# The scans' solve on two diagonal blocks, on opposite quarters of the array

## The chip, the cores and the metric

One core of one Trainium2 chip runs the kernel. The metric is the device time of one execution, in microseconds. The kernel before took 3053.93 us (median of three runs, 3050.66 to 3057.09).

## The reference, cut to what matters

The reference is a two-layer backbone over 512 tokens (256 of context, 256 latent), 1024 wide, in fp32. Each layer projects its input, runs four token mixers, merges them and applies a feed-forward part (dense in layer 0, eight experts in layer 1). One of the four mixers scans the tokens with a state of 64 x 64 for each of four heads, once forward and once backward:

```python
def step(state, inp):
    r_t, w_t, k_t, v_t, a_t, b_t = inp
    sa = jnp.einsum('bhvk,bhk->bhv', state, a_t)
    state = (state * w_t[:, :, None, :] + sa[..., None] * b_t[:, :, None, :]
             + v_t[..., None] * k_t[:, :, None, :])
    return state, jnp.einsum('bhvk,bhk->bhv', state, r_t)
```

Only this scan is touched. The context's tokens are scanned first; layer 1 needs outputs y of the latent tokens alone.

## The kernel before, in words

The scan is done in chunks of 128 tokens: 4 chunks by 2 directions give the 8 groups of a layer, 16 in the kernel. In a chunk the token's dependence on earlier tokens of the same chunk is a strictly triangular 128 x 128 matrix A for each head, and what is wanted is the inverse of 1 - A, applied to a right side of 64 columns. A is split into "near" (blocks of 16 on the diagonal, D) and "far" (the rest, E0). The inverse of the near part is a product of powers, F = (1+D)(1+D^2)(1+D^4)(1+D^8), and that of what is left is G = (1+Z)(1+Z^2)(1+Z^4), with Z the far part times F. The vectors u0 (right side), u1 = F u0 and u = G u1 follow from the state of the chunk before; from u follow the next state and the outputs y.

All of it is written out by hand, as one fixed order of instructions on each of three engines, with a semaphore value for each step (`done`/`tick`). The four heads are numbered p + 2q: p picks 64 of 128 partitions where a head is an operand's rows, and one of two banks of PSUM where it is an output, so that most steps come twice, for p = 0 and p = 1.

- TensorE (`solve`, line 689; all matrix products stand in the trace under line 465, the transposes under 745): the gram products of the chunk (bank 0/1: b with a and r; bank 4/5: a with b; bank 2/3: k with a and r, after `carry_u0` of the group before); then D^2, D^4 and F2, D^8 and F3, F4, four transposes of b and k, Z, Z^2, Z^4 and G2, G3. Between these stand the steps of the group before: `carry_u0` (line 622), `carry_u1`, `carry_u` and `carry_state` (state and y). `four` multiplies two heads of one p, 128 x 128 by 128 x 128. One fp32 product is two MATMUL records in the trace, each with a weight load of its own.
- VectorE (`solve`, line 1891): masks of the gram products (lines 1907 to 1919, with 1912 for 1 + D), the sums of F and G (line 1925), 1 + Z (line 1945), the copies of u0 and u, the state (lines 1872, 1873), the output y (lines 1885, 1887). In groups 0 to 3 it also prepares the second direction (`sums`, `rates`, `hats`), in groups 6 and 7 it splits weights for the stage after.
- ScalarE (`solve`, line 1389): copies of every squared matrix from PSUM to SBUF, one per p (128x512 for D^2, D^4, Z, Z^2; 128x256 for D^8, Z^4), the turned b and k, and u1; the exponentials of the second direction after groups 1 and 2.

SyncE loads the weights in order through a ring of four units; three of its units serve as scratch until `hats` of the second direction. What follows the scans (`attention_in`) waits for "group end" of group 7. The masks come with the constants, 128 x 128 each.

## Time and profile before

| what | value |
|---|---|
| time, median of three runs | 3053.93 us |
| the profiled execution's own time | 3055.04 us |
| its span in the trace | 3053.2 us |
| TensorE busy, whole span | 2920.9 us (96%) |
| scans of layer 0 | 111 to 313 us of the span |
| scans of layer 1 | 1368 to 1558 us of the span |
| in the 202 us of layer 0's scans: TensorE, VectorE, ScalarE busy | 192.57, 121.79, 66.75 us |

The profile is one execution. "Busy" counts an engine's instructions; of TensorE the weight loads are listed apart (PEld), and they overlap the products. PEclk is the share of full clock that TensorE was granted: 1.00 is 2.4 GHz, 0.50 is 1.2 GHz. The time outside the two scans is not touched by the change.

### The profile page before, as it was taken

The page shows a single profiled execution, that of the slowest core. Times are in us where ns is not written, and L with a number is a line of the kernel's source. Part 1 is how long each engine was busy: PE and PEld are TensorE (multiplying, and loading weights), DVE is VectorE, ACT ScalarE, POOL GpSimd, SP SyncE. Part 2 cuts the span into 40 slices and gives each one's busy share as a digit, 9 for nine tenths or more (in the row PEclk, how much of TensorE's full clock was granted, in tenths as well). Part 3 has the DMA queues.
Part 4 walks back from the last instruction along what each step waited for, and adds up shares of the span by engine and source line. Part 5 has one row for each costly group of instructions (what it writes and reads, how often), then busy time and mean ns, then how long its engine had stood idle before and what let it go on. Part 6 is the DMA issues. An engine that isn't in the chain of part 4 may idle for free.

```text
span 3053.2 us, 43457 instructions
## 1 busy us (share of the span) xinstructions
PE 2920.9 (96%) x16364; PEld 2406.1 (79%) x16364; DVE 1980.7 (65%) x2592; ACT 1577.7 (52%) x2073; POOL 0.2 (0%) x4
## 2 busy tenths in 40 slices
PE   7999999999899999899999898999999999999997
PEld 4788676787688878669887797888888888888886
DVE  3765575335422233476556556988988889888887
ACT  5433446223322222353344544777777777777775
POOL 0000000000000000000000000000000000000000
PEclk8999999999999999999999998999999999999999
DMA  6010136223122222200114454899998999989995
GB/s 254 1 43 1 55 140 222 95 97 118 70 97 97 97 83 97 83 14 1 43 42 160 174 181 167 339 351 354 352 347 342 355 356 349 348 341 355 357 348 212
DMA packets 79820, 575.53 MB, mean 188 GB/s; under 512 B 8896, under 2 KB 10176, under 8 KB 10176
## 3 DMA queue, kind: packets, MB, share of 16 engines
q1 hardware_dynamic: 78960, 568.49, 49.4%
q10 hardware_dynamic: 720, 5.08, 0.4%
q8 instruction: 99, 1.62, 0.2%
q14 instruction: 41, 0.34, 0.0%
HBM read 572.49 MB, written 1.05 MB: 188 GB/s over the span
## 4 chain that ended last, share of the span: by engine, by line
PE 86%; DVE 8%; ACT 3%; issue 2%; DMA 0%; DVEq 0%; ACTq 0%; SPq 0%
PE bank L465 84%; PE bank L1122 1%; PE bank L961 1%; ACT weights_high L1213 1%; DVE weights_low L2179 1%; ACT hT L1213 1%; DVE weights_low L1720 1%; ACT more_weights_high L1213 1%; ACT arena L1213 1%; DVE arena L1992 1%; DVE arena L1763 0%; DVE arena L1925 0%; DMA xT<-xin 0%; DVE arena L1696 0%; DVE arena L1750 0%
## 5 line engine op out<-in xcount | busy, mean ns | idle before, releaser
L1213 ACT ACTIVATE arena<-bank 128x512 f32<-128x512 f32 (+2 forms) x647 | 310.9, 491 | 871.0 <-PE bank L465 780.8
L1213 ACT ACTIVATE weights_high<-ring 128x1024 fp32r<-128x1024 f32 (+1 forms) x366 | 508.5, 1397 | 313.2 <-PE bank L465 312.7
L1720 DVE TENSOR_TENSOR weights_low<-ring,weights_high 128x1024 fp32r<-128x1024 f32 x220 | 266.2, 1224 | 399.4 <-ACT weights_high L1213 399.3
L465 PE MATMUL bank<-arena 128*128 128x128 f32 (+6 forms) x3632 | 453.4, 297 | 23.1 <-DVE arena L1925 6.0
L465 PEld LDWEIGHTS bank<-arena 128*128 128x128 f32 (+3 forms) x3632 | 390.1, 182 | 64.8 <-issue 23.8
L2179 DVE TENSOR_TENSOR weights_low<-ring,weights_high 128x2048 fp32r<-128x2048 f32 x146 | 334.6, 2292 | 66.1 <-ACT weights_high L1213 65.8
L465 PE MATMUL bank<-h_low,weights_high 128*128 128x512 f32 (+1 forms) x960 | 348.3, 363 | 0.0
L465 PE MATMUL bank<-weights_high,tokens_high 128*128 128x512 f32 x684 | 276.2, 404 | 7.2 <-DVE weights_low L2179 5.5
L465 PE MATMUL bank<-weights_high,tokens_low 128*128 128x512 f32 x684 | 267.6, 391 | 0.0
L2179 DVE TENSOR_TENSOR more_weights_low<-arena,weights_high 128x2048 fp32r<-128x2048 f32 x108 | 247.6, 2292 | 30.5 <-ACT weights_high L1213 30.3
L1213 ACT ACTIVATE weights_high<-arena 128x2048 fp32r<-128x2048 f32 x108 | 207.0, 1917 | 44.7 <-PE bank L465 44.7
L465 PE MATMUL bank<-weights_low,tokens_high 128*128 128x512 f32 x576 | 224.5, 390 | 0.0
L465 PEld LDWEIGHTS bank<-h_low,weights_high 128*128 128x128 f32 x960 | 182.8, 190 | 27.0
L465 PE MATMUL bank<-h_high_ffn,weights_high 128*128 128x512 f32 x448 | 176.0, 393 | 10.1 <-DVE h_low L1727 10.1
L465 PE MATMUL bank<-h_high_gates,weights_high 128*128 128x512 f32 (+1 forms) x512 | 174.0, 340 | 9.0 <-DVE h_low L1727 9.0
L2179 DVE TENSOR_TENSOR weights_low<-ring,more_weights_high 128x2048 fp32r<-128x2048 f32 x73 | 167.4, 2293 | 18.7 <-ACT more_weights_high L1213 18.5
L465 PE MATMUL bank<-h_high_ffn,weights_low 128*128 128x512 f32 x448 | 175.0, 391 | 0.0
L465 PE MATMUL bank<-h_high_gates,weights_low 128*128 128x512 f32 (+1 forms) x512 | 173.0, 338 | 0.0
L465 PE MATMUL bank<-more_weights_low,tokens_high 128*128 128x512 f32 x432 | 168.5, 390 | 0.0
L465 PEld LDWEIGHTS bank<-weights_high,tokens_high 128*128 128x128 f32 x684 | 128.4, 188 | 36.0 <-DVE weights_low L2179 9.3
L1213 ACT ACTIVATE more_weights_high<-ring 128x2048 fp32r<-128x2048 f32 x73 | 139.8, 1915 | 26.2 <-PE bank L465 26.2
L465 PEld LDWEIGHTS bank<-weights_high,tokens_low 128*128 128x128 f32 x684 | 128.3, 188 | 27.9
(282 smaller groups left out, 5439.9 us busy)
## 6 DMA issues: line engine op xcount, KB each, us to landing
ring<-wstream SPq DMA_DIRECT2D x377, 1024.0 KB, 4.8
arena<-wstream SPq DMA_DIRECT2D x162, 1024.0 KB, 4.8
sm<-small ACTq DMA_DIRECT2D x2, 1568.0 KB, 8.8
xT<-xin SPq DMA_DIRECT2D x1, 2048.0 KB, 9.4
cn<-consts ACTq DMA_DIRECT2D x1, 1732.0 KB, 7.0
out<-hT SPq DMA_DIRECT2D x2, 512.0 KB, 3.0
vec<-vecs SPq DMA_DIRECT2D x1, 121.5 KB, 2.4
cn<-consts ACTq DMA_DIRECT2D x1, 65.0 KB, 2.5
```

Source lines behind the costliest of these rows:

```text
L465: return nc.tensor.matmul(o, lhsT, rhs, start=first, stop=last)
L961: ins = nc.tensor.transpose(bank[4 + s][:, b * P:(b + 1) * P], T(PB[n % 3 * 2 + s])[:, b * P:(b + 1) * P], C("ident"))
L1122: ins = nc.tensor.transpose(bank[5 - 3 * (p % 2)][:, c * P:(c + 1) * P], ghid[:, p % 2, c * P:(c + 1) * P], C("ident"))
L1213: return nc.scalar.activation(o, i, func, **kw)
L1720: step(vx.tensor_tensor(ring_low[:, u % RING, cols], ring[:, u % RING, cols], wh[:, j % 4, :].bitcast(F32), ALU.subtract), "weights low", j)
L1992: chain(vx.reciprocal(r, r))
L2179: return vx.tensor_tensor(low, raw, moe_high(q).bitcast(F32), ALU.subtract)
```

## The change

The chunk's matrix is taken as two by two blocks of 64. Only the two diagonal blocks of a head are inverted, and the block that couples the second half of the tokens to the first is applied apart.

- `four` now takes all four heads: for each head and each half s, 64 x 64 by 64 x 64, with operands on the partitions of half s and the output on the same partitions. That is 8 products instead of 2 (4 over both p), and all tiles hold the four heads side by side, so each step has one wait, one copy and one sum in place of two (by p).
- In a block of 64 the series of G ends one factor earlier: Z^4 and G3 are gone, and Z^2 is made in one orientation.
- The gram products a with b are made in 64 x 64 pieces, 16 of them in both orientations, and 4 more for the coupling block C; b with r and k with a, r stay as they are. They are issued at the end of the group before (`gram_blocks`).
- New on TensorE: FC (F times C), W (FC times G), and the product of W with the first half of u (`carry_across`), whose result VectorE adds to the second half of u. u1 and u are made with 8 products of 64 x 64 each, not 4 of 128 x 128. G2 of a group is made at the start of the next group's `solve`.
- ScalarE copies C, FC and W (64 partitions), and one tile each for D^2, D^4, D^8, Z, Z^2.
- The output y goes to bank 1 and is made after FC, apart from the state; VectorE takes it in the next but one `solve`. `sums` is cut in two parts, and `hats` now stands before 1 + Z ("G1") of groups 2 and 3 instead of behind it.
- The masks near and far are 64 wide, and a 64 x 64 identity on both halves is new.

The core of the diff, with lines that only rename or move left out:

```diff
-        def half_tiles(i):
-            return T(i, 2).rearrange("p a (k h t) -> p a k h t", k=2, h=2)
-        DD = half_tiles(M_)
-        D2 = half_tiles(M_ + 2)
-        FG_of = (half_tiles(FG_), half_tiles(FG_ + 2))
-        AR2_of = (half_tiles(AR2_), half_tiles(AR2_ + 2))
...
-        E0 = two_halves(E0_)
-        E1_of = (two_halves(E1_), two_halves(E1_ + 1))
-        D8 = two_halves(D8_)
+        def whole(i):
+            return T(i).rearrange("p (h t) -> p h t", h=4)
+        def blocks(i):
+            return T(i).rearrange("p (k h t) -> p k h t", k=2, h=4)
+        DD, D2, FW = blocks(M_), blocks(M_ + 1), blocks(M_ + 2)
+        FG_of = (blocks(FG_), blocks(FG_ + 1))
+        EC, D8 = blocks(E0_), blocks(D8_)[:, 0]
+        E1_of = (whole(E1_), whole(E1_ + 1))
+        AR2_of = ((whole(AR2_), whole(AR2_ + 1)), (whole(AR2_ + 2), whole(AR2_ + 3)))
+        def ends(d):
+            return (rows(0), rows(1)) if d == 0 else (rows(1), rows(0))
         bk_of = (T(BK_), T(BK_ + 1))
...
-            def four(o, left, right, kind):
-                for q in range(2):
-                    ins = mm(o[:, (2 * kind + q) * P:(2 * kind + q + 1) * P], left[:, q, :], right[:, q, :])
+            def four(o, left, right):
+                for h in range(4):
+                    for s in range(2):
+                        ins = mm(o[rows(s), h * HD:(h + 1) * HD], left[rows(s), h, :], right[rows(s), h, :])
+                return ins
+            def across(o, to, left, right, of):
+                for h in range(4):
+                    ins = mm(o[to, h * HD:(h + 1) * HD], left[of, h, :], right[of, h, :])
                 return ins
...
-                        ins = mm(bank[6 + p][:, P + q * HD:P + (q + 1) * HD], FG_of[m % 2][:, p, 0, q, :], u0[:, p, q, :])
+                        for s in range(2):
+                            ins = mm(bank[6 + p][rows(s), P + q * HD:P + (q + 1) * HD],
+                                     FG_of[m % 2][rows(s), 0, 2 * p + q, :], u0[rows(s), p, q, :])
...
+            def carry_across(l, m):
+                first, second = ends(groups[m][0])
+                pe.wait_ge(*done("W", l, m))
+                for p in range(2):
+                    pe.wait_ge(*done("u", l, m, p))
+                    for q in range(2):
+                        ins = mm(bank[6 + p][second, P + q * HD:P + (q + 1) * HD], FW[first, 1, 2 * p + q, :],
+                                 uu[first, p, q, :])
+                    ins.then_inc(*tick(products, "u across product", l, m, p))
...
+            def gram_blocks(l, n):
                 d, c = groups[n]
-                cols = slice(c * CH, (c + 1) * CH)
-                FG = FG_of[n % 2]
+                first, second = ends(d)
+                def of_chunk(part_):
+                    return slice(c * CH + part_.start, c * CH + part_.stop)
                 if n % 4 == 0:
                     pe.wait_ge(*done("hats", l, d, 1))
                 if n == 0:
                     pe.wait_ge(*done("rate read", l, 1, 1))
+                for kind in range(2):
+                    for q in range(2):
+                        for p in range(2):
+                            for s in range(2):
+                                a, b = ar_of[d][rows(p), q, c, 0, rows(s)], bh(d, q)[rows(p), of_chunk(rows(s))]
+                                at = 2 * kind + q
+                                ins = mm(bank[4 + p][rows(s), at * HD:(at + 1) * HD], *((b, a) if kind else (a, b)))
+                ins.then_inc(*tick(products, "gram", l, n))
+                if n:
+                    pe.wait_ge(*done("bk", l, n - 1))
+                    pe.wait_ge(*done("FC", l, n - 1))
                 for q in range(2):
                     for p in range(2):
-                        mm(bank[p][:].rearrange("p (s q t) -> p q s t", s=2, q=2)[:, q], bh(d, q)[rows(p), cols],
-                           ar_of[d][rows(p), q, c, :, :])
+                        ins = mm(bank[2 + p][second, (4 + q) * HD:(5 + q) * HD], ar_of[d][rows(p), q, c, 0, second],
+                                 bh(d, q)[rows(p), of_chunk(first)])
+                ins.then_inc(*tick(products, "gram across", l, n))
...
+            def last_power(l, n):
+                pe.wait_ge(*done("Z2", l, n))
+                pe.wait_ge(*done("G1", l, n))
+                four(bank[0][:, 256:512], D2[:, 1], FG_of[n % 2][:, 1]).then_inc(*tick(products, "G2 product", l, n))
+            def across_second(l, n):
+                first, second = ends(groups[n][0])
+                pe.wait_ge(*done("G2", l, n))
+                pe.wait_ge(*done("FC", l, n))
+                across(bank[3], first, FW[:, 0], FG_of[n % 2][:, 1], second).then_inc(*tick(products, "W product", l, n))
+            def solve(l, n):
+                d, c = groups[n]
+                first, second = ends(d)
+                FG = FG_of[n % 2]
+                cols = slice(c * CH, (c + 1) * CH)
+                if n == 0:
+                    gram_blocks(l, 0)
+                else:
+                    last_power(l, n - 1)
+                    carry_u0(l, n - 1)
+                pe.wait_ge(*done("masked D", l, n))
+                pe.wait_ge(*done("C", l, n))
+                four(bank[4][:, 0:256], DD[:, 1], DD[:, 0])
+                four(bank[4][:, 256:512], DD[:, 0], DD[:, 1]).then_inc(*tick(products, "D2 product", l, n))
+                if n:
+                    across_second(l, n - 1)
+                    carry_u1(l, n - 1)
+                pe.wait_ge(*done("D2", l, n))
+                four(bank[5][:, 0:256], D2[:, 1], D2[:, 0])
+                four(bank[5][:, 256:512], D2[:, 0], D2[:, 1]).then_inc(*tick(products, "D4 product", l, n))
+                pe.wait_ge(*done("F1", l, n))
+                four(bank[4][:, 256:512], D2[:, 0], FG[:, 0]).then_inc(*tick(products, "F2 product", l, n))
+                if n >= 2:
+                    pe.wait_ge(*done("group end", l, n - 2))
                 for q in range(2):
                     for p in range(2):
+                        ins = mm(bank[p][:, q * P:(q + 1) * P], bh(d, q)[rows(p), cols], ar_of[d][rows(p), q, c, 1, :])
+                ins.then_inc(*tick(products, "gram r", l, n))
                 if n:
+                    pe.wait_ge(*done("W", l, n - 1))
                 for q in range(2):
                     for p in range(2):
                         ins = mm(bank[2 + p][:, 2 * q * P:2 * q * P + 2 * P], kh(d, q)[rows(p), cols],
                                  ar_of[d][rows(p), q, c, :, :])
+                ins.then_inc(*tick(products, "gram k", l, n))
                 if n:
                     carry_u(l, n - 1)
+                pe.wait_ge(*done("D4", l, n))
+                pe.wait_ge(*done("F2", l, n))
+                four(bank[4], DD[:, 1], DD[:, 0]).then_inc(*tick(products, "D8 product", l, n))
+                four(bank[5], DD[:, 0], FG[:, 0]).then_inc(*tick(products, "F3 product", l, n))
                 if n:
+                    carry_across(l, n - 1)
+                pe.wait_ge(*done("D8", l, n))
+                pe.wait_ge(*done("F3", l, n))
+                four(bank[4][:, 256:512], D8, FG[:, 0]).then_inc(*tick(products, "F4 product", l, n))
+                pe.wait_ge(*done("masked k", l, n, 0))
                 for i in range(4):
                     ins = nc.tensor.transpose(bank[2][:, i * P:(i + 1) * P],
                                               (bh(d, i) if i < 2 else kh(d, i - 2))[:, cols], C("ident"))
                 ins.then_inc(*tick(products, "bk turned", l, n))
+                if n:
+                    carry_state(l, n - 1)
+                pe.wait_ge(*done("F4", l, n))
+                four(bank[5][:, 0:256], EC[:, 0], FG[:, 0])
+                four(bank[5][:, 256:512], FG[:, 0], EC[:, 0]).then_inc(*tick(products, "Z product", l, n))
+                pe.wait_ge(*done("masked k", l, n, 1))
+                across(bank[3], second, FG[:, 0], EC[:, 1], second).then_inc(*tick(products, "FC product", l, n))
+                if n:
+                    carry_y(l, n - 1)
+                pe.wait_ge(*done("Z", l, n))
+                pe.wait_ge(*done("masked r", l, n))
+                four(bank[0], DD[:, 0], DD[:, 1]).then_inc(*tick(products, "Z2 product", l, n))
+                if n < 7:
+                    gram_blocks(l, n + 1)
...
+                def across(n):
+                    _, second = ends(groups[n][0])
+                    act.wait_ge(*done("gram across", l, n))
+                    for p in range(2):
+                        ins = f(EC[second, 1, 2 * p:2 * p + 2], bank[2 + p][second, 256:384]
+                                .rearrange("p (q t) -> p q t", q=2), ACT.Copy)
+                    ins.then_inc(*tick(scalars, "C", l, n))
+                def across_second(n):
+                    first, _ = ends(groups[n][0])
+                    copy(FW[first, 1], by_head(3, 0, first), ("W", "W product"), n)
                 def solve(n):
+                    _, second = ends(groups[n][0])
+                    if n == 0:
+                        across(0)
+                    copy(D2, both_kinds(4), ("D2", "D2 product"), n)
                     if n:
+                        across_second(n - 1)
                         carry_u1(n - 1)
+                    act.wait_ge(*done("F1", l, n))
+                    copy(DD, both_kinds(5), ("D4", "D4 product"), n)
+                    copy(D8, by_head(4), ("D8", "D8 product"), n)
                     act.wait_ge(*done("bk turned", l, n))
                     if n == 0:
                         act.wait_ge(*done("hats", l, 0, 1))
                     if n >= 2 and n != 5:
                         act.wait_ge(*done("state product", l, n - 2, 1))
                     f(bk_of[n % 2], bank[2][:], ACT.Copy).then_inc(*tick(scalars, "bk", l, n))
+                    copy(DD, both_kinds(5), ("Z", "Z product"), n)
+                    copy(FW[second, 0], by_head(3, 0, second), ("FC", "FC product"), n)
+                    copy(D2[:, 1], by_head(0), ("Z2", "Z2 product"), n)
+                    if n < 7:
+                        across(n + 1)
...
+            def mask_blocks(l, n):
+                up, low = ways(groups[n][0])
+                dve.wait_ge(*done("gram", l, n))
+                if n:
+                    dve.wait_ge(*done("G1", l, n - 1))
+                for p in range(2):
+                    own_heads = slice(2 * p, 2 * p + 2)
+                    x = bank[4 + p][:, 0:256].rearrange("p (k q t) -> p k q t", k=2, q=2)
+                    vx.tensor_tensor(DD[:, 0, own_heads], x[:, 0], mask("near" + low, HD, 2), ALU.mult)
+                    vx.tensor_tensor(DD[:, 1, own_heads], x[:, 1], mask("near" + up, HD, 2), ALU.mult)
+                    vx.tensor_tensor(EC[:, 0, own_heads], x[:, 0], mask("far" + low, HD, 2), ALU.mult)                        .then_inc(*tick(vectors, "masked D", l, n))
+                dve.wait_ge(*done("masked D", l, n))
+                step(vx.tensor_tensor(FG_of[n % 2][:, 0], DD[:, 1], mask("eye64"), ALU.add), "F1", l, n)
...
             def solve(l, n):
+                if n == 0:
+                    mask_blocks(l, 0)
+                else:
+                    add(l, n - 1, 1, 0, 256, "G2")
                     carry_u0(l, n - 1)
+                if n >= 2:
+                    carry_y(l, n - 2)
+                if n < 2:
+                    running_sums(l, 1, n)
+                add(l, n, 0, 4, 256, "F2")
+                mask_r(l, n)
+                mask_k(l, n, 0)
                 if n:
                     carry_u(l, n - 1)
+                add(l, n, 0, 5, 0, "F3")
+                if n:
+                    carry_across(l, n - 1)
+                add(l, n, 0, 4, 256, "F4")
+                mask_k(l, n, 1)
+                if n < 2:
+                    centred_sums(l, 1, n)
+                elif n < 4:
+                    rates(l, 1, n - 2)
+                    hats(l, 1, n - 2)
+                elif n >= 6:
+                    weights_low(LAYER_START[l] + ATT_AT + 2 * n - 10)
+                dve.wait_ge(*done("Z", l, n))
+                step(vx.tensor_tensor(FG_of[n % 2][:, 1], DD[:, 0], mask("eye64"), ALU.add), "G1", l, n)
                 if n:
                     carry_state(l, n - 1)
+                if n < 7:
+                    mask_blocks(l, n + 1)
```

## Rows read from the trace of the kernel before

**Rows 1.** The page, parts 1 and 4: busy time by engine, chain by engine.
```profile
PE 2920.9 (96%) x16364; PEld 2406.1 (79%) x16364; DVE 1980.7 (65%) x2592; ACT 1577.7 (52%) x2073; POOL 0.2 (0%) x4
...
PE 86%; DVE 8%; ACT 3%; issue 2%; DMA 0%; DVEq 0%; ACTq 0%; SPq 0%
```

**Rows 2.** Busy time by window (us, records); both layers' scans, then three short stretches.
```profile
core 0: us, PE busy (x) PEld busy (x) DVE busy (x) ACT busy (x) POOL busy (x), PEclk, DMA share, GB/s
111.00:313.00 202.00, 192.57 (x1729) 174.08 (x1729) 121.79 (x333) 66.75 (x133) 0.00 (x0) 0.96 0.04 17
1368.00:1559.00 191.00, 183.57 (x1634) 168.03 (x1635) 117.90 (x325) 67.55 (x134) 0.00 (x0) 0.97 0.05 18
...
112.00:116.00 4.00, 4.00 (x24) 2.89 (x21) 1.65 (x6) 0.00 (x0) 0.00 (x0) 0.50 0.00 0
...
300.00:313.00 13.00, 11.08 (x74) 8.91 (x73) 3.66 (x11) 1.13 (x5) 0.00 (x0) 0.68 0.00 1
1537.47:1539.47 2.00, 2.00 (x35) 1.42 (x36) 0.58 (x2) 0.05 (x1) 0.00 (x0) 1.00 0.00 0
```

**Rows 3.** Timeline (start us, length us): first mask of groups 5 and 6.
```profile
232.02 0.42 DVE L1907 TENSOR_TENSOR arena<-bank,cn 128x256 f32<-128x256 f32 x1 [1.15 <-PE bank L465]
...
255.97 0.42 DVE L1907 TENSOR_TENSOR arena<-bank,cn 128x256 f32<-128x256 f32 x1 [1.15 <-PE bank L465]
```

**Rows 4.** Groups of instructions by form, 231 to 255 us (busy, mean ns, idle before).
```profile
L465 PE MATMUL bank<-arena 128*128 128x128 f32 x120 | 15.0, 280 | 0.5 <-DVE arena L1925 0.5
L1213 ACT ACTIVATE arena<-bank 128x512 f32<-128x512 f32 x9 | 5.4, 597 | 14.4 <-PE bank L465 10.3 <-PE bank L745 4.1
L1925 DVE TENSOR_TENSOR arena<-arena,bank 128x256 f32<-128x256 f32 x10 | 4.1, 420 | 6.5 <-PE bank L465 6.4
...
L1213 ACT ACTIVATE arena<-bank 128x256 f32<-128x256 f32 x4 | 1.5, 384 | 2.2 <-PE bank L465 2.2
```

**Rows 5.** Timeline of weight loads in group 5, a load beside each product record.
```profile
231.65 0.31 PEld L465 LDWEIGHTS bank<-state,arena 64*128 64x128 f32 x4
...
232.02 0.52 PEld L465 LDWEIGHTS bank<-arena 128*128 128x128 f32 x4
...
232.61 0.30 PEld L465 LDWEIGHTS bank<-state,arena 64*128 64x128 f32 x4
...
237.30 2.76 PEld L465 LDWEIGHTS bank<-arena 128*128 128x128 f32 x24
...
239.98 0.97 PEld L465 LDWEIGHTS bank<-u,arena 128*128 128x128 f32 x8
...
242.87 0.20 PEld L465 LDWEIGHTS bank<-uu,arena 128*64 128x64 f32 x4
...
243.48 0.19 PEld L465 LDWEIGHTS bank<-arena,state 64*64 64x64 f32 x4
...
243.84 0.20 PEld L465 LDWEIGHTS bank<-arena,uu 128*64 128x64 f32 x4 [0.17 <-issue]
...
244.43 0.19 PEld L465 LDWEIGHTS bank<-arena,state 64*64 64x64 f32 x4 [0.17 <-issue]
...
245.39 0.97 PEld L465 LDWEIGHTS bank<-arena 128*128 128x128 f32 x8 [0.17 <-issue]
```

**Rows 6.** The same view at the gram products of group 6.
```profile
254.29 1.39 PEld L465 LDWEIGHTS bank<-arena 64*128 64x128 f32 x16
255.60 0.19 PEld L465 LDWEIGHTS bank<-state,arena 64*128 64x128 f32 x2
```

**Rows 7.** Timeline in group 2: the end of `hats`, TensorE's next load.
```profile
179.71 0.68 DVE L1840 TENSOR_TENSOR arena<-ring 128x512 f32<-128x512 f32 x1
...
180.92 0.75 PEld L465 LDWEIGHTS bank<-arena 128*128 128x128 f32 x6 [1.80 <-ACT ring L1213]
```

**Rows 8.** TensorE's sequencer at two waits (lines 763, 630), first and last start us.
```profile
L763 PEldq EVENT_SEMAPHORE  x1: 51/51/51, 253.6 to 253.6; - x1
...
L630 PEldq EVENT_SEMAPHORE  x1: 51/51/51, 254.3 to 254.3; - x1
```

210 lines of the change are left out of this document (71 added, 139 removed), and 2 rows, old and new, of the table _n.

## The prediction

> **What bounds the kernel now.** First the page: TensorE is busy 96% of the span and holds 86% of the chain that ended last [rows 1]. Then the windows of the two scans: of 202 us in layer 0 TensorE is busy 193, VectorE 122, ScalarE 67, and layer 1 looks alike [rows 2]. So inside the scans, too, time goes by TensorE's work. Then the pace: from the first mask of one group to that of the next 255.97 - 232.02 = 23.95 us [rows 3]. By form, 120 of a group's records are 128 x 128 by 128 x 128, and TensorE sits idle 0.5 us before them, while ScalarE waits 14.4 us and VectorE 6.5 us for TensorE [rows 4]. The reader should see that these two are the followers, and have room.
>
> **The unit costs**, by start to start of weight loads:
> - A record over the full array: 24 of them from 237.30 to 239.98, 0.112 us each [rows 5].
> - The outputs of y: 4 records of 64*64 in 243.84 - 243.48 = 0.36, then 8 of 128*64 in 0.59 [rows 5]. The second stretch has two pairs more, so a pair with 128 columns costs 0.11 and a change of layout (which part of the array a weight fills) 0.36 - 0.22 = 0.14. The four 64*64 loads stand within 0.19 us: the two opposite quarters run side by side, like the column halves.
> - 16 records of 128*64 with 64 columns take 243.48 - 242.87 = 0.61, less one change 0.47 for eight pairs: 0.059 a pair [rows 5]. I call that a slot.
> - u0: twice 232.61 - 231.65, 1.92, with four changes in it [rows 5]. Sixteen gram records 1.31: four pairs of 128 columns 0.44, so four pairs of 256 columns 0.87 [rows 6].
>
> On a change of layout the Trainium skill, "TensorEngine Tiling (Array Packing)", section "Key Properties", says that changing the mode drains the array; it gives no price, and the 0.14 above is what it costs here.
>
> **A group before**, on TensorE: 136 full records (120 of the solve, 16 of u1 and u) 15.2; u0 1.92; gram products 0.44 + 0.87 + 0.87; four transposes 0.44; state 0.61; y with its changes 1.91; three more changes 0.4: 22.7. The other 1.3 of 23.95 are waits and edges.
>
> **A group after.** Slots with two quarters: G2 8, D^2 16, u1 8, D^4 16, F2 8, u 8, D^8 8, F3 8, F4 8, Z 16, Z^2 8, gram blocks 16, coupling gram 4: 132. Steps on one quarter alone (W, FC, the product across) are 24 records, each of which I price as a slot too, since each column half above advanced by one record in 0.059. Nothing in the trace shows one quarter alone; bounds are 0.03 (it pairs with a neighbour) and 0.112 (a full record), and the half-width row is the nearest. So 156 slots, 9.2 us. No row has this form with 64 columns either: for the 132 the lower bound is 0.055 (half of the 0.11 for 128 columns) and the upper one two full records, 0.224; I take 0.059, because the same-width weights of rows 5 show it and because the quarters ran side by side there.
> Kept: u0 1.92, gram r 0.44, gram k 0.87, transposes 0.44, state 0.47 without its change, y 1.91: 6.05. Layout changes not in these: into u0, into and out of the r and k grams, into the transposes, into the state, into Z and one for the edge of a 128-wide load: 7 x 0.14 = 1.0. Sum 16.25 us, 6.4 less than 22.7.
>
> **Which waits come.** An answer of ScalarE costs TensorE the tail of the last record (mean 280 ns less the slot, about 0.17 [rows 4]), the copy (0.60, or 0.38 for half), and about 0.1 for the two semaphores: 0.86 or 0.64; a sum on VectorE 0.42 + 0.27, about 0.68 [rows 4].
> - D^2 copy 0.86, beside it W and u1, 0.94: covered, by 0.08 only. If it is not, it costs at most 0.9.
> - D^4 copy 0.86, beside F2, both grams and u, over 2.3. F4's sum 0.68, beside transposes and state, 1.2. Z's copy 0.86, beside FC and y, 2.4 (FC alone where layer 1 has no y: 0.4 late). Z^2's copy 0.64, beside the gram blocks, 1.2. The masks of the next group, 1.4 on VectorE and its 0.27, beside G2 and u0, 2.5.
> - F3's sum 0.68, beside the product across, 0.47: 0.2 late in every group. This is the new stall.
> VectorE's work falls from 15.2 us a group (121.79 by 8, rows 2) to about 11.4, ScalarE's from 8.3 to 6.1: neither becomes the bound at 16.4.
> So a steady group is 16.45 instead of 23.95: 7.5 saved. In layer 1, where four groups make no y and both versions lose about 1.9 less the wait for Z, it is 6.9.
>
> Groups 2 and 3: VectorE does 2.7 us of rates and now also the 2.7 us of hats before G1. Before, TensorE already lost time there: hats ended at 179.71 + 0.68, the next load came at 180.92 after 1.80 idle [rows 7]. In the new order G1 ends about 0.8 us after TensorE wants it, and the state behind G1 costs u0 another 0.8: 18.1 against 25.6 (22.8 for layer 1's group 2 before). The two first groups have nothing of a group before to cover the waits with: here the sums by p of the old order covered each other, the single ones of the new do not, and I get 13.9 against 19.0. The rest of group 7 with the tail after it (G2, u0, W, u1, u, across, y, each waiting for the one before) loses the old solve's work and gains the link across: 24.8 against 29.9, the start of group 0 counted in.
> Following TensorE's order step by step with these prices, the other two engines beside it, I get for layer 0 between the starts of D^2 of successive groups 13.9, 16.4, 18.2, 18.0, 15.8, 16.4, 16.4 and a tail; for layer 1 13.9, 15.0, 18.2, 18.0, 15.8, 15.0, 15.1. The old order followed alike gives 19.0, 24.5, 25.5, 25.5, 22.5, 23.7, 23.7 (rows 3 have 23.95 for such a last one) and 19.0, 21.8, 22.9, 25.5, 22.5, 21.8, 21.8. With 5.1 for the tails the differences are 54.3 + 49.3, about 103 us in all. Nothing else hangs on it: the stages behind wait for the end of group 7 and move up whole, the ring is full by then but for three scratch units that are free from group 3 on.
>
> The execution of this profile took 3055.0 us (span 3053.2, 1.8 around it), 1.1 over the median. 3055.0 - 103 = **2952 us**.
>
> **The rivals.**
> 1. *TensorE's issue is the floor.* The new group has 364 records where the old has 220, and they come in runs of a hundred at 0.03 us each. The trace has no such run. At the end of a group 20 records (4 of G3, 16 gram) are issued between the sequencer's waits at 253.6 and 254.3: 0.03 to 0.04 each, with room in its queue not known [rows 8]. At 0.035 to 0.04 the slot is 0.07 to 0.08, which saves 84 to 65: 2971 to 2990.
> 2. *The other side: the quarters don't run side by side, or records pass one by one.* Then a slot is two records. The densest 2 us of the trace hold 35 records, 0.057 each, and the burst at 0.03 above could be one that had queued up behind the change of layout [rows 2, 5]. Slot 0.114: +3, no change. Slot 0.124: a group is 132 x 0.124 + 24 x 0.062 + 7.05 = 24.9, +25 in all, 3080 us. It decides from a slot of 0.112 on, a full record. Against it: the 0.19 us of the four 64*64 loads.
> The Trainium skill, "TensorE: Matmul & The Clock Gate", section "Wait — 56ns, not 53.3ns?", says that the sequencer spends about 62 ns on each matmul where hardware decoding is off. By that rule the time would be the 3080 of this rival; the burst of sixteen in 0.47 us and rows 8 speak against it.
> 3. *The clock.* At the start of the scans TensorE has 0.50 of its clock while it catches up, and 0.68 over the last 13 us, where it waits for one vector after another [rows 2]. If the small weights and more short waits brought it to 1.2 GHz inside the groups as well, TensorE's work would take up to twice as long: 32 us a group, 8 over the old one, 3055 + 16 x 8 = 3183; half of the time at that level gives 24.2 a group and about 3059, the point from which it is slower. Against it: the idle 1.80 us of rows 7 cost no clock (0.96 over the scans), and the new order's waits inside a group are 0.2.
> 4. *A wait that my walk misses* (W or the masks late by a step, 3 us in each of 16 groups): 2952 + 48 = 3000.
>
> **Chances.** Forecast 0.70 (2935 to 2975, from a slot of 0.055 and gram blocks that run on four quarters at once, 7 us less, to one of 0.07); rival 1 0.12; rival 2 0.07; rival 3 0.05; rival 4 0.06. Range 2935 to 3000. About 0.2% (6 us) is what a measurement of this kernel can tell from no change. Faster: 0.70 + 0.12 + 0.06 and 0.01 of rival 2; same 0.02; slower 0.09.
>
> **What would show it.** The first masks of successive late groups 16.4 us apart; 16 records of a `four` in about 0.47 us; TensorE idle 0.2 before F4 and about 1.6 in groups 2 and 3, nothing before D^4; scans of about 147 us (layer 0) and 140 us (layer 1); the rest of the trace the same length. Wrong if a `four` takes 0.6 or more (rival 1) or 0.9 or more (rival 2), if the granted clock over the scans is under 0.9 (rival 3), or if TensorE's idle time inside a late group is over 1 us (rival 4).

## The result, and the profile after

The changed kernel takes 2940.05 us (median of four runs, 2938.77 to 2942.70), the kernel before beside it 3052.3 us: ratio 0.963, interval 0.961 to 0.965, 112 us saved. The forecast was 2952, a saving of 103. The profiled spans differ as the runs do: 3053.2 - 2940.9 = 112.3 us.

The page after, parts 1 and 4 (as [rows 1]):

```profile
PE 2800.5 (95%) x18668; PEld 2288.3 (78%) x18668; DVE 1923.8 (65%) x2496; ACT 1534.9 (52%) x2025; POOL 0.2 (0%) x4
...
PE 85%; DVE 8%; ACT 4%; issue 2%; DMA 0%; DVEq 0%; ACTq 0%; SPq 0%
```

TensorE has 2304 records more, 144 a group as forecast, and is busy 120 us less: more and smaller records in less time. It still bounds the kernel.

Windows after (us; busy and records of PE, PEld, DVE, ACT, POOL; granted clock, DMA): scans of layer 0, scans of layer 1, the first group, one steady group, a stretch in layer 1 behind group 3's start, and layer 0's last group with its tail (as [rows 2]):

```profile
109.00:252.00 143.00, 129.62 (x2883) 111.81 (x2883) 95.09 (x289) 46.82 (x111) 0.00 (x0) 0.96 0.07 25
1302.00:1444.00 142.00, 126.21 (x2786) 110.28 (x2787) 91.36 (x279) 46.12 (x110) 0.00 (x0) 0.92 0.07 25
...
112.40:127.70 15.30, 12.78 (x255) 11.30 (x252) 8.69 (x26) 3.97 (x9) 0.00 (x0) 0.71 0.01 2
214.67:230.60 15.93, 15.49 (x364) 13.48 (x364) 11.39 (x34) 6.56 (x15) 0.00 (x0) 1.00 0.02 3
...
1354.00:1361.00 7.00, 7.00 (x120) 6.81 (x120) 1.43 (x6) 1.85 (x5) 0.00 (x0) 0.56 0.01 2
226.55:251.10 24.55, 21.49 (x426) 17.89 (x420) 15.00 (x46) 7.34 (x17) 0.00 (x0) 1.00 0.01 3
```

A steady group holds the 364 records of the forecast and is 15.93 us long. The clock is full inside it; it is low in the first group, after the long wait of layer 1's group 3, and in part of layer 1's tail (0.91 over its group 7 and tail).

The first masks of groups 6 and 7, timeline of VectorE, start and length in us (as [rows 3]):

```profile
210.61 0.29 DVE L2001 TENSOR_TENSOR arena<-bank,cn 128x128 f32<-128x128 f32 x1
...
226.55 0.29 DVE L2001 TENSOR_TENSOR arena<-bank,cn 128x128 f32<-128x128 f32 x1
```

226.55 - 210.61 = 15.94, where [rows 3] have 23.95. All such intervals, from start of the masks to start of the masks, forecast beside measured:

| | groups 0 to 6 | sum | group 7 and tail |
|---|---|---|---|
| layer 0 before | 18.71 24.90 25.62 25.62 22.72 23.95 23.96 | 165.5 | 32.86 |
| after | 15.26 16.19 17.91 17.67 15.01 16.18 15.93 | 114.2 | 24.56 |
| forecast after | 13.9 16.4 18.2 18.0 15.8 16.4 16.4 | 115.1 | 24.8 |
| layer 1 before | 18.61 22.07 22.79 25.62 22.72 22.02 22.02 | 155.9 | 31.35 |
| after | 14.56 15.04 17.68 20.32 14.90 15.04 14.90 | 112.4 | 25.77 |
| forecast after | 13.9 15.0 18.2 18.0 15.8 15.0 15.1 | 111.0 | 24.8 |

The weight loads of the steady group, in order, from D^4 to the next D^4; in brackets the idle time before and what ended it (as [rows 5]):

```profile
214.67 2.72 PEld L469 LDWEIGHTS bank<-arena 64*64 64x64 f32 x64 [0.25 <-ACT arena L1276]
217.73 0.54 PEld L469 LDWEIGHTS bank<-u,arena 64*64 64x64 f32 x16 [0.33 <-issue]
218.19 0.90 PEld L469 LDWEIGHTS bank<-arena 64*64 64x64 f32 x28
218.95 0.13 PEld L469 LDWEIGHTS bank<-uu,arena 64*64 64x64 f32 x1
...
219.93 0.57 PEld L469 LDWEIGHTS bank<-arena 64*64 64x64 f32 x16 [0.43 <-issue]
220.57 0.42 PEld L809 LDWEIGHTS bank<-cn,arena 128*128 128x128 f32 x4
221.15 0.20 PEld L469 LDWEIGHTS bank<-uu,arena 128*64 128x64 f32 x4 [0.17 <-DVE arena L2010]
...
225.07 1.71 PEld L469 LDWEIGHTS bank<-arena 64*64 64x64 f32 x72 [0.17 <-issue]
226.85 0.30 PEld L469 LDWEIGHTS bank<-state,arena 64*128 64x128 f32 x4
...
228.17 1.77 PEld L469 LDWEIGHTS bank<-arena 128*128 128x128 f32 x42
229.81 0.19 PEld L469 LDWEIGHTS bank<-u,arena 64*64 64x64 f32 x3
...
230.60 0.20 PEld L469 LDWEIGHTS bank<-arena 64*64 64x64 f32 x4 [0.25 <-ACT arena L1276]
```

Read it as a ledger. A line joins loads of the same names, so its label is the first one's form. F4's 16 records stand from 219.93 to 220.57, with a change of layout behind them: 0.64, forecast 0.47 + 0.14. The line of 72 from 225.07 is Z^2, the gram blocks, the coupling gram and G2: 1.78 to the next line. Two idle times of TensorE are new: 0.25 before D^4 and 0.43 before F4. The 0.33 before u is no stop, since the products ahead of it run on until 217.80, and the 0.17 at changes of layout stand in [rows 5] too.

### The profile page after: what moved, and what is told of

Read it like the earlier page. It is cut to its first block, busy times and chain, and to the rows that moved or that the text cites. A ratio compares the mean times of both kernels' runs of the same rounds, so it can differ in the third digit from the quotient of the medians.

```text
span 2940.9 us, 47827 instructions
## 1 busy us (share of the span) xinstructions
PE 2800.5 (95%) x18668; PEld 2288.3 (78%) x18668; DVE 1923.8 (65%) x2496; ACT 1534.9 (52%) x2025; POOL 0.2 (0%) x4
## 3 DMA queue, kind: packets, MB, share of 16 engines
q8 instruction: 117, 1.92, 0.3%
## 4 chain that ended last, share of the span: by engine, by line
PE 85%; DVE 8%; ACT 4%; issue 2%; DMA 0%; DVEq 0%; ACTq 0%; SPq 0%
PE bank L469 83%; ACT arena L1276 1%; PE bank L1185 1%; PE bank L1024 1%; ACT weights_high L1276 1%; DVE weights_low L1798 1%; ACT hT L1276 1%; DVE weights_low L2293 1%; ACT more_weights_high L1276 1%; DVE arena L2106 1%; DVE arena L1841 0%; DMA xT<-xin 0%; PE bank L809 0%; DVE arena L1774 0%; DVE arena L1828 0%
## 5 line engine op out<-in xcount | busy, mean ns | idle before, releaser
L1276 ACT ACTIVATE arena<-bank 128x256 f32<-128x256 f32 (+4 forms) x599 | 269.1, 463 | 813.7 <-PE bank L469 743.0
L469 PE MATMUL bank<-arena 64*64 64x64 f32 (+7 forms) x5296 | 340.7, 253 | 27.8 <-DVE arena L2010 5.8
L469 PEld LDWEIGHTS bank<-arena 64*64 64x64 f32 (+4 forms) x5296 | 282.0, 150 | 64.6 <-issue 23.9
```

The lines of the kernel that those rows point to most:

```text
L469: return nc.tensor.matmul(o, lhsT, rhs, start=first, stop=last)
L1276: return nc.scalar.activation(o, i, func, **kw)
```

## The experiments

Each was run beside the kernel before; times are compared with the changed kernel's 2940.05. The kernel before took 3054.4 to 3055.0 us in these comparisons and 3052.3 in the first, so 2 or 3 us between runs of different comparisons tell nothing.

**Are the opposite quarters what saves?** `four` without alternation:

```diff
-                for h in range(4):
-                    for s in range(2):
+                for s in range(2):
+                    for h in range(4):
```

> The changed kernel, but each `four` issues its four products on one quarter and then its four on the opposite quarter, instead of alternating. 12 such steps a group. Theory A (the gain is the two quarters side by side, and only neighbours in the order run so): a `four` takes 16 x 0.059 = 0.94 us instead of 0.47, 12 x 0.47 = 5.6 us a group, some of it in place of waits, so +75 to +90 us, about 3020 us. Theory B (TensorE's queue finds the free quarter further down the order by itself, as it seems to when the eight records of W start within the last pairs of D^2): no change, 2940 us. In between (it looks ahead by fewer records than the eight of one quarter): +15 to +45 us.

Measured: 2980.85 us, 41 us more, ratio to before 0.976 (0.975 to 0.978). A late group is 18.2 us. F4 in this kernel, the same view, with the transposes behind it:

```profile
233.35 0.82 PEld L469 LDWEIGHTS bank<-arena 64*64 64x64 f32 x16 [0.43 <-issue]
234.24 0.42 PEld L809 LDWEIGHTS bank<-cn,arena 128*128 128x128 f32 x4
```

234.24 - 233.35 = 0.89 where the changed kernel has 0.64. With 0.17 off for the layout that is 0.72 for 16 records: 0.47 if all pair up, 0.93 if none does. So somewhat over half of the overlap is lost, not all: by start times (single records, not shown), the second quarter's first load starts at 233.63, when six of the first's eight have started, and its first product when three of the first's are still to come. Neither pure case holds. If this share of the overlap is worth 41 us, all of it is worth some 65 to 75, an estimate from 0.72 (and from the 0.69 between the first and the last load's start, 0.40 if all pair up and 0.87 if none does). The quarters do run side by side, TensorE takes up later records past ones that wait for their own quarter, and it does so over a short distance only.

**How much comes from fewer steps?** The kernel before, its products at full size, without Z^4, G3 and one orientation of Z^2, and with the gram products put in another order, so that the ones that overwrite G2's bank wait for it; its output lacks those factors of the series (the order of the gram products is left out here):

```diff
-                    four(bank[p], DD[:, p, 1], DD[:, p, 0], 0)
                     four(bank[p], DD[:, p, 0], DD[:, p, 1], 1)...
-                    four(bank[4 + p], D2[:, p, 0], D2[:, p, 1], 0)...
...
-                    four(bank[2 + p], D8[:, p], FG[:, p, 1], 0)...
```

> The kernel before, with its 128 x 128 products kept, but the series of G one factor shorter: Z^4, G3 and one orientation of Z^2 are left out (so part of the inverse of the far part is not computed). It tells how much of the gain is fewer steps and how much is the quarters. 24 records of 0.112 go, 2.7 us a group, and a new wait for G2 at the next gram products costs about 0.25: 2.4 x 16 = 39 us less, 3013 us. So the quarters would hold some 70 of the 112 us. Rival: TensorE's order is held by the waits for the other engines, not by its records, and the shorter series gives under 20 us.

Measured: 3031.34 us against 3054.43 beside it, 23 us less, ratio 0.993 (0.991 to 0.995). Late groups are 1.6 to 2.3 us shorter. The groups 3 are 25.35 and 27.52, 0.3 shorter and 1.9 longer; the granted clock over them is 0.95 and 0.88, where the kernel before has 1.00. A part of what took back the rest shows in the weight loads in group 5, waits that the removed products had covered:

```profile
220.89 0.97 PEld L465 LDWEIGHTS bank<-arena 128*128 128x128 f32 x8 [0.37 <-ACT arena L1207]
222.08 1.96 PEld L465 LDWEIGHTS bank<-arena 128*128 128x128 f32 x20 [0.22 <-ACT arena L1207]
```

So the shorter series gives between 23 us (as it is) and the 39 expected, which had one wait of 0.25 in it. The 73 to 89 of the 112 that are left belong to the quarters and to what came with them (y behind FC, below, about 10). No run takes the quarters alone away; apart, by its 41 us and the 65 to 75 worked out from it, agrees with a share of that size.

**Are the changes of layout priced right?** One full-array product more ahead of D^4, D^8 and F4; nothing reads it:

```diff
+                extra(bank[5][:, 0:HD])
                 four(bank[5][:, 0:256], D2[:, 1], D2[:, 0])
```

> The changed kernel with one more product over the full array (two records, 64 columns, result overwritten) ahead of D^4, of D^8 and of F4, each between two steps on quarters: two more changes of layout each time. If a change costs 0.14 us as read before, each place costs 2 x 0.11 + 2 x 0.14 + up to 0.05 = 0.5 to 0.55 us, three places in 16 groups +25 us, 2966 us. Rival: the drain hides behind the neighbours' tails, and only the records cost: +10 us, 2951 us.

Measured: 2961.00 us, 21 more (0.970, 0.968 to 0.971). Most groups are 1.20 to 1.23 us longer, 0.40 a place. In the weight loads, at D^4 and before D^8:

```profile
237.56 0.30 PEld L469 LDWEIGHTS bank<-cn 128*128 128x128 f32 x2 [0.25 <-ACT arena L1282]
237.93 2.72 PEld L469 LDWEIGHTS bank<-arena 64*64 64x64 f32 x64
...
241.60 0.30 PEld L469 LDWEIGHTS bank<-cn 128*128 128x128 f32 x2
241.96 0.89 PEld L469 LDWEIGHTS bank<-arena 64*64 64x64 f32 x28
```

The product's two records with the change behind them take 0.37. Two records over the full array advance by 0.22 [rows 5], which leaves 0.15 for that change. At D^4 and F4 the change ahead of the product adds nothing, since TensorE stands still there anyway. At D^8 it does: from u's first load to D^8's is 241.96 - 240.99 = 0.97, where the changed kernel has 218.19 - 217.73 = 0.46, so 0.51 for the product with two changes. 0.37 + 0.51 + 0.37 = 1.25 a group, the 1.2 measured. The 0.14 of the prediction stands, and where a wait stands at the same place it hides in it.

**Does y cover something?** y right behind the state, as in the kernel before:

```diff
                     carry_state(l, n - 1)
+                    carry_y(l, n - 1)
                 pe.wait_ge(*done("F4", l, n))
```

> The changed kernel with the output y made right behind the state again, not behind FC. Theory of the cover: the copy of Z (0.86 us from the last record to the next load) then has only FC beside it (0.35 to 0.47), so about 0.45 us of new idle time in each of the 12 groups with a y, +5 us, 2945 us; the trace shows TensorE idle before Z^2 by about 0.4. Rival: the wait is taken up elsewhere, since y now covers the sum of F4 that transposes and state cover already: no change, idle time before Z^2 but as much less before other steps.

Measured: 2950.27 us, 10 more (0.966, 0.964 to 0.968). Late groups with y are 0.5 to 0.8 longer (layer 0's groups 2 and 3 are 0.2 shorter and 1.2 longer). The loads of Z and FC, and of Z^2 behind them, in a late group:

```profile
225.31 1.47 PEld L469 LDWEIGHTS bank<-arena 64*64 64x64 f32 x40 [0.17 <-issue]
227.15 1.71 PEld L469 LDWEIGHTS bank<-arena 64*64 64x64 f32 x72 [0.37 <-ACT arena L1275]
```

With y gone from behind FC, Z's copy is waited for, 0.37, as the prediction had it for groups without y (0.4). Over both layers the intervals sum to 3.7 us more, which is this wait and its edges. The tail of layer 0 is 2.4 longer, and there this profile's clock is at half for a part (0.87 over the last group with its tail, where the changed kernel has 1.00); that of layer 1 is 0.9 shorter. The remaining 5 us of the median I can't place, so the time confirms the cover only in its direction; the wait of 0.37 confirms it in size.

**Do four quarters run at once in the gram blocks?**

```diff
-                for kind in range(2):
-                    for q in range(2):
+                for other in range(2):
+                    for kind, q in ((0, 0), (0, 1), (1, 0), (1, 1)):
                         for p in range(2):
-                            for s in range(2):
+                            for s in ((p + other) % 2,):
```

> The changed kernel with the 16 products of the gram blocks in another order: two opposite quarters at a time (first the two on the diagonal for all four outputs, then the other two) and not four quarters in turn. Theory A: the gram blocks take 0.52 us and not the forecast 0.94 because four quarters run at once; then they take 0.94 here, each group is 0.42 us longer, and the time is 2940 + 16 x 0.42 = 2947. Rival B: their short time is hidden beside Z^2's copy, which the next step waits for anyway, or a quarter's rate does not depend on its neighbours: 2940 or 2941.

Measured: 2943.26 us, ratio 0.963 (0.962 to 0.965): not told apart from the changed kernel. The late groups 5 and 6 of layer 0 are 16.06 and 16.06 by the profile, where the changed kernel has 16.18 and 15.93: the same together. The stretch of 72 records in them:

```profile
226.66 1.83 PEld L469 LDWEIGHTS bank<-arena 64*64 64x64 f32 x72 [0.17 <-issue]
228.56 0.30 PEld L469 LDWEIGHTS bank<-state,arena 64*128 64x128 f32 x4
```

1.90 against 1.78. Theory A fails: the gain is not tied to four quarters in turn. That four quarters do run at once in the changed kernel its single loads show (not printed here): 30 of the gram's 32 start between 225.47 and 225.89, 0.014 each, where one quarter alone starts one in 0.0585. In the order of pairs the gram's first half follows Z^2 on the diagonal, and its second half, on the other two quarters, starts (227.42) before the first has ended (227.53) and runs on beside the coupling gram and G2. What counts is, in the main, how many records the busiest quarter gets. In this stretch that is Z^2 8, gram 8, coupling 4, G2 8: 28 by 0.0585 = 1.64, and 0.14 for the layout 1.78, which is what the changed kernel takes; pairs has the same count and takes 0.12 more. The prediction counted 36 slots, 2.12.

The rival's first half, that the gram's short time hides beside Z^2's copy, is not excluded. G2 needs that copy, and in the changed kernel both ends fall together. The copy and G2 behind it, in layer 1's group 2:

```profile
1333.62 0.38 ACT L1276 ACTIVATE arena<-bank 128x256 f32<-128x256 f32 x1 [0.38 <-PE bank L469]
...
1334.05 0.55 PEld L469 LDWEIGHTS bank<-arena 64*64 64x64 f32 x16
```

G2's first load comes 0.05 behind the copy's end, as D^4's at 214.67 comes 0.05 behind the end of D^2's copy; and the 20 slots from Z^2's first load, 1332.89, end at 1334.06. So a still faster gram would have gained nothing here. In pairs the copy ends at 227.77 and G2 starts at 227.95: there the quarters hold it.

**VectorE's work in groups 2 and 3, and the clock.** In layer 1's group 3 of the changed kernel, TensorE's loads and VectorE's work before them:

```profile
1347.45 0.54 PEld L469 LDWEIGHTS bank<-arena 64*64 64x64 f32 x15 [0.37 <-ACT arena L1276]
1351.09 0.57 PEld L469 LDWEIGHTS bank<-arena 64*64 64x64 f32 x16 [2.39 <-ACT ring L1276]
1352.39 0.33 PEld L469 LDWEIGHTS bank<-state,scan_room 64*128 64x128 f32 x4 [0.73 <-DVE state L1966]
```

```profile
1345.52 0.54 DVE L1904 TENSOR_SCALAR ring<-ring,vec,omka 128x512 f32<-128x512 f32 x1
...
1349.96 0.68 DVE L1925 TENSOR_TENSOR arena<-ring 128x512 f32<-128x512 f32 x1
1350.56 0.41 DVE L2057 TENSOR_TENSOR arena<-arena,cn 128x256 f32<-128x256 f32 x1
```

The load at 1351.09 is G2; the row names ScalarE, which had long been done, and what ended last is VectorE's G1 (line 2057, to 1350.97), behind 5 us of rates and hats. At 1353.4 the clock goes to half, for 6.8 us. Two edits, apart, together, and one with the fill at the head alone:

```diff
hats:
                 if n < 2:
                     running_sums(l, 1, n)
+                elif n < 4:
+                    rates(l, 1, n - 2)
                 add(l, n, 0, 4, 256, "F2")
...
                 elif n < 4:
-                    rates(l, 1, n - 2)
                     hats(l, 1, n - 2)
fill:
+                pe.wait_ge(*done("f0", l, IN_ORDER[4]))
+                fill(3)
                 turn_v(l)
+                fill(6)
...
                 pe.wait_ge(*done("Z2", l, n))
+                if n in (2, 3):
+                    fill(4, 256)
```

`fill(k)` is k products of 128 x 128 by 128 x 256 that nothing reads.

> The changed kernel with products that nothing reads (128 x 128 by 128 x 256, into a bank that is free) put in front of TensorE's long waits: 9 at the head of each layer's scans, 4 before the last power of groups 2 and 3, where TensorE waits for VectorE's hats. Theory A: what the idle stretches cost beyond their own length is the clock, which fell to half behind them (at 107.5 and 1353.4 us in the changed kernel's profile). Then the granted clock stays at 1.00 in layer 1's group 3, whose interval goes from 20.3 to 17.7 us, and the head of layer 0 gets 1 to 3 us shorter: 4 to 9 us in all, 2931 to 2936. Rival B: the long interval of layer 1's group 3 is VectorE's work and not the clock's; it stays at 20.3, and the time at 2940 or some us above.

> The changed kernel with the rates of groups 2 and 3 (2.7 us of VectorE) moved to the earlier slot, before F2's sum, where groups 0 and 1 have their running sums; the hats stay ahead of G1. Theory A: in groups 2 and 3 TensorE waits for VectorE's rates and hats before G1 and for the state behind it; with half of that gone from there the intervals of groups 2 and 3 fall from 17.7 to 16.2 or 16.4 us, four times, and layer 1's group 3 also gets back the 2.6 us of the clock: 2940 - 6 - 3 = 2931. Rival B: the rates then hold up F2's sum and TensorE waits there instead: intervals of 17.5 or more, 2940.

> Both of these edits at once: the idle products ahead of the long waits and the rates in the earlier slot. If the two gains are of different kinds (VectorE's work, and the clock at the head), they add: 2925 to 2930. If both only keep the clock from falling in layer 1's group 3, it comes out like the better one alone, 2931.

> The kernel with the rates in the earlier slot (run hats), and of the products that nothing reads only the 9 at the head of each layer's scans. In run fill these shortened layer 0's first interval from 15.3 to 12.3 us while the 4 before the last powers added 1.6 and 1.9 us to the group behind groups 2 and 3. Theory A: the head's gain stands by itself, 2.2 us at least on top of run hats: 2927 to 2930, under every other kernel here. Rival B: the clock's low stretch moves to a later place and gives the gain back: 2931 to 2934.

> The changed kernel as it is, once more, beside the kernel of run head: its ratio to the kernel before should be 0.963 as in the first comparison, 2940 to 2943, so that runs hats, fill, pairs and head can be held against it within 2 us.

| kernel | us | ratio to before, interval | first group, layer 0 | groups 2, 3 | layer 1: 2, 3 | 4 (both layers) |
|---|---|---|---|---|---|---|
| changed | 2940.05 | 0.963, 0.961 to 0.965 | 15.26 | 17.91 17.67 | 17.68 20.32 | 15.01 14.90 |
| again | 2939.68 | 0.963, 0.962 to 0.964 | 14.55 | 17.92 17.68 | 17.67 19.91 | 15.01 15.15 |
| fill | 2943.30 | 0.963, 0.962 to 0.965 | 12.27 | 17.91 18.01 | 17.67 20.30 | 16.56 16.78 |
| hats | 2931.53 | 0.960, 0.958 to 0.961 | 14.49 | 15.94 15.95 | 15.04 15.71 | 15.64 15.14 |
| both | 2939.92 | 0.962, 0.960 to 0.963 | 12.27 | 15.94 18.02 | 15.04 17.22 | 17.20 17.20 |
| head | 2932.84 | 0.959, 0.958 to 0.961 | 12.27 | 15.94 15.94 | 15.04 15.70 | 15.26 16.32 |

- *hats* does what its theory says: 2931.5 where 2931 was expected. That the size fits so well is in part luck: the groups give 10.8 us, not 9, and the two tails take back 2.0 and 1.0, at granted clocks of 0.87 and 0.84 over the last groups with their tails (1.00 and 0.91 in the changed kernel). Group 2 gets 2.0 (layer 0) and 2.6 us shorter, group 3 1.7 and 4.6. In layer 1's group 3 TensorE's wait of 2.39 is gone, and the low clock behind it too (in hats, where that group starts at 1350.5; the clock is the number before the last two):

```profile
1346.00:1353.00 7.00, 6.28 (x160) 5.70 (x158) 6.80 (x24) 4.07 (x10) 0.00 (x0) 1.00 0.02 5
1353.00:1361.00 8.00, 7.56 (x193) 6.63 (x188) 6.34 (x16) 2.23 (x7) 0.00 (x0) 1.00 0.01 2
```

Groups 4 give back 0.6 and 0.2.
- *fill* does not confirm the clock as its theory had it. The windows from 107 to 122 us in the changed kernel and in fill:

```profile
107.00:122.00 15.00, 10.88 (x156) 9.51 (x158) 9.60 (x25) 3.54 (x8) 0.00 (x0) 0.54 0.00 1
```

```profile
107.00:122.00 15.00, 12.52 (x249) 10.78 (x248) 11.71 (x31) 3.97 (x10) 0.00 (x0) 1.00 0.01 2
1302.00:1318.00 16.00, 13.28 (x302) 11.91 (x295) 9.70 (x31) 4.41 (x11) 0.00 (x0) 0.79 0.01 3
1346.00:1353.00 7.00, 6.02 (x78) 4.91 (x71) 6.53 (x21) 2.50 (x7) 0.00 (x0) 0.88 0.01 2
1353.00:1361.00 8.00, 8.00 (x169) 7.50 (x166) 2.33 (x7) 2.08 (x6) 0.00 (x0) 0.68 0.01 2
```

At the head of layer 0 it holds: clock 1.00 for 0.54, and 3.0 us less in the first group (2.3 less than in again). At the head of layer 1 the same nine products bring nothing: 14.80 for 14.56. In layer 1's group 3 the clock fell all the same, although TensorE's wait had shrunk from 2.39 to 0.67 us, and the interval stayed at 20.3. And the fill itself, four products in 1.6 us (1346.49 to 1348.08), holds up the group behind by 1.6 and 1.9 us. Together that is nothing gained. So the rival's number came, 20.3, but not by its cause: the clock alone accounts for what layer 1's group 3 has over layer 0's 17.67, which is at full clock. Three profiles have much the same waits at its start (2.39 and 0.73 us; 2.40 and 0.48; 2.11 and 0.73) and half clock for different times behind them. Group 3 of layer 1 in the changed kernel, in again and in pairs:

```profile
1352.35:1372.67 20.32, 18.55 (x364) 16.39 (x364) 13.44 (x38) 4.62 (x12) 0.00 (x0) 0.83 0.05 8
```

```profile
1349.00:1368.91 19.91, 18.13 (x364) 15.83 (x364) 13.45 (x39) 4.55 (x12) 0.00 (x0) 0.85 0.05 8
```

```profile
1357.81:1376.62 18.81, 17.16 (x364) 15.05 (x364) 13.35 (x38) 4.60 (x12) 0.00 (x0) 0.91 0.06 10
```

The missing 0.17, 0.15 and 0.09 of the clock are 6.8, 5.8 and 3.4 us at half clock, and the group is 2.65, 2.24 and 1.14 us over 17.67: 0.34 to 0.39 us for each us at half clock. What brought the clock down is not shown by this; in hats the wait and the fall are gone together.
- *both*: the fills stand where no wait is left to cover them, 2.1 and 1.5 us more in the groups 3 than in hats, 1.6 and 2.1 in the groups 4.
- *head* keeps the gain of the first group (12.27, 2.2 less than hats), and its median is that of hats, as its rival had it. That the low clock moved to a later place is not shown: layer 0's tail is long in both (26.64 and 26.58), layer 1's group 4 is 1.2 longer and its tail 2.5 shorter than in hats.
- *again* gives the same time as the first comparison. Its profiled span is 2935.3, 5.6 shorter than the other profile of the same kernel. Of this 3.3 us lie between the two scans; inside them the first groups (0.7 shorter, 1.2 longer), layer 1's group 3 (0.4 shorter) and its tail (24.33 for 25.77, with no half clock in it) differ. Such a stretch moves by 1 us or so from one execution to the next with the clock's low stretches.

hats and head both beat the changed kernel, by some 8 us (0.3%): the slowest of their ten runs, 2936.7, is under the fastest of its nine, 2937.2. They are not told apart from each other.

## Why the prediction was right

**The mechanism was right, and the groups came out as worked out.** Records a group, 0.059 a slot (measured 0.0585: D^2's 32 records in 0.93 us), TensorE as the bound with VectorE at 11.39 and ScalarE at 6.56 us of 15.93 (forecast 11.4 and 6.1). Rival 1 (issue at 0.035 to 0.04 a record) and rival 2 (one by one) are out: the 72 records of the line at 225.07 start 1.57 us apart, first to last, 0.022 each. The 62 ns a matmul that the Trainium skill gives for one way of decoding ("TensorE: Matmul & The Clock Gate", "Wait — 56ns, not 53.3ns?") is not what this kernel pays; whether it uses that way of decoding no run shows. Rival 3 did not come (clock 0.96 and 0.92 over the scans), rival 4 neither. Rival 1's price doesn't follow from its own slot: at 0.07 and 0.08 the 132 slots with two quarters cost 23 and 44 us more, which gives 2975 (the figure that the forecast's own upper end has) and 2996, not 2971 and 2990.

The steady group by the ledger, start to start:

| stretch | forecast | measured |
|---|---|---|
| D^4, F2, layout | 1.42 + 0.14 | 1.55 |
| gram r, gram k, layout | 1.31 + 0.14 | 1.51 |
| u, D8, F3, across, wait for F4 | 1.42 + 0.47 + 0.2 | 2.20 |
| F4, layout | 0.61 | 0.64 |
| transposes, layout | 0.58 | 0.58 |
| state, layout | 0.61 | 0.62 |
| Z, FC, y | 0.94 + 0.47 + 1.91 | 3.30 |
| Z^2, gram blocks, coupling, G2, layout | 2.12 + 0.14 | 1.78 |
| u0 | 1.92 | 1.91 |
| D^2, W, u1 | 0.94 + 0.94 | 1.84 |
| sum | 16.28 (16.45 with one edge of 0.14 more, and rounding) | 15.93 |

**Mis-sized terms inside the group.**
- *Gram blocks and their neighbours*: 36 slots for two quarters, 28 in fact. The prediction named this as the lower bound (7 us over all) and did not take it; 0.48 x 16 is 7.7 us. The reason is that four quarters run at once; pairs shows that it need not be four in turn, and Z^2's copy would have ended a larger gain.
- *The single-quarter steps*, a slot for each record: right for FC, which lies on the quarter that its neighbours use. W and the product across lie on a quarter that is free, so they slide in beside what runs (W's first load stands at 229.52, D^2's last at 229.63; across starts at 218.95 amid F3's records). That gives no time back here, since what they were to cover is then bare: this is where the 0.25 before D^4 comes from (the cover was called short "by 0.08 only") and why the wait for F4 is 0.43 and not 0.2.
- *Groups 2 and 3*: forecast 18.2 and 18.0, measured 17.9 and 17.7; 20.32 in layer 1's group 3, where the clock fell. hats confirms that VectorE's rates and hats set them. TensorE's idle time in the two waits (G1, then the state) was forecast as about 1.6 and is 1.66 and 1.69 in layer 0; in layer 1 it is 3.12 and 1.69, the longer one where no y stands ahead of it.
- *First groups*: 13.9 forecast, 15.26 and 14.56 measured. The forecast priced them at full clock, the trace has 0.71 over the first; with the clock kept up it takes 12.27. So the price was 1.6 too high, the clock added 3.0, and the one hides the other.

These nearly cancel, which is luck: the intervals after sum to 226.6 us, forecast 226.1.

**Where the 9 us more came from.** The intervals gave 94.7 us (forecast 93.4). Group 7 with the tail gave 8.3 + 5.6, and layer 0's first mask comes 2.1 us sooner, 1.8 of it because the first gram is shorter (1.20 us from its first load to the mask, not 2.96): the step "24.8 against 29.9, the start of group 0 counted in", 10.2 us for both layers, was the one mis-sized. Its new side was right (24.56 and 25.77, the second with half clock in it; 24.33 in again without). Its old side was my walk at full clock, while the trace had 32.86 and 31.35 us, with a clock of 0.68 over the last 13 us [rows 2]: 4.4 us. The number stood in the trace and was not read. Of the rest, 4.0 us came between the end of layer 0's scans and the first mask of layer 1, 1.8 of it layer 1's shorter first gram, and 2.4 were lost behind layer 1. What is left of these two is of the size by which two profiles of the same kernel differ (3.3 us between the scans, above), and I leave it there.

## What to carry to other kernels

For small products, count the records of each quarter of the array and price a stretch by its busiest one (0.0585 us for 64 columns in fp32, two records a product), which came out to within 0.12 us for 72 records here; look beside it for the copy that the next step needs; order issues so that neighbours fall on different quarters, since TensorE looks past a waiting record only a little way. A step that slides beside another no longer covers a copy: look for its wait in the next step. And when a saving is worked out, take the old side from the trace's rows, the ends of a loop too, and not from the model that gives the new side.

## What the runs showed of the hardware

- Two records on different quarters start 7 ns apart, a run of 72 goes at 0.022 us each, and 30 on four quarters at 0.014; a quarter by itself takes a record of 64 columns every 0.0585.
- A product over the full array amid 64 x 64 ones costs 0.51 us, 0.37 where it stands behind a wait, and 0.22 among its like.
- Nine products that nothing reads kept the clock of layer 0's first group at 1.00 and shortened it by 2.2 to 3.0 us, and layer 1's by nothing; the whole kernel was not faster for it in any of the three runs with them (fill, both, head).
- In layer 1's group 3, each us at half clock cost 0.34 to 0.39 us of the group (3.4, 5.8 and 6.8 us in three profiles).
- In layer 1's group 3, waits of 0.67 and 0.82 us with G2 between them were followed by half clock in fill; one of 0.60 there, in hats, was not.
